# Sliding-window attention in a four-layer encoder: row sums of half the heads on VectorE instead of ScalarE's accumulator

## The reference, cut to what matters

```python
def swa_sink_mixer(h, w_in, sinks, w_out):
    ...
    s = jnp.einsum('bcqhgd,bckhd->bhgcqk', qc, kb) * (SW_HEAD ** -0.5)
    s = jnp.where(valid[:, None, :], s, -jnp.inf)
    sink = sinks.astype(F32).reshape(SW_KV_HEADS, SW_GROUP)[None, :, :, None, None, None]
    m = jnp.maximum(jnp.max(s, axis=-1, keepdims=True), sink)
    p = jnp.exp(s - m)
    p = p / (jnp.sum(p, axis=-1, keepdims=True) + jnp.exp(sink - m))
    o = jnp.einsum('bhgcqk,bckhd->bcqhgd', p, vb).reshape(B, T, SW_WIDTH)
    o = o * jax.nn.silu(g.astype(F32))
    return o.astype(h.dtype) @ w_out
```

## Time and profile before

| | |
|---|---|
| median of 3 runs | 1368.39 us |
| the profiled execution, its own time | 1368.35 us |
| its span, first to last instruction | 1366.5 us |
| TensorE busy | 1302.6 us, 95% |
| VectorE busy | 770.8 us, 56% |
| ScalarE busy | 429.2 us, 31% |
| GpSimd busy | 176.4 us, 13% |
| mean granted TensorE clock | 0.99 |

### The profile page before, as it was taken

How to read it: one execution, slowest core, us unless ns; L and a number is a source line. 1 busy time by engine, 2 the same in 40 slices (tenths; PEclk the granted TensorE clock), 3 DMA queues, 4 the chain that set the end, 5 groups by cost and what they waited for, 6 DMA issues and landing times. The chain is left out here.

```text
span 1366.5 us, 24895 instructions
## 1 busy us (share of the span) xinstructions
PE 1302.6 (95%) x10657; PEld 747.8 (55%) x10657; DVE 770.8 (56%) x1478; ACT 429.2 (31%) x1013; POOL 176.4 (13%) x168
## 2 busy tenths in 40 slices
PE   5999999999999999879999999899999999999998
PEld 3444444478746998754544446445444444468743
DVE  5676785966653333585444014424676785966653
ACT  3124166035302002561312062502123266035401
POOL 0000152010030243133000020000000153000000
PEclk9999999999999999989999999999999999999999
DMA  7222222100420223410222221113322222100221
GB/s 224 78 62 61 70 70 62 47 3 4 171 81 0 78 78 93 148 39 0 59 62 77 77 62 47 47 62 114 108 64 62 62 67 74 47 3 4 96 110 62
DMA packets 122270, 93.44 MB, mean 68 GB/s; under 512 B 5096, under 2 KB 112016, under 8 KB 121648
## 3 DMA queue, kind: packets, MB, share of 16 engines
q1 hardware_dynamic: 121456, 89.71, 21.9%
q10 hardware_dynamic: 704, 2.13, 0.4%
HBM read 85.54 MB, written 6.29 MB: 67 GB/s over the span
## 5 line engine op out<-in xcount | busy, mean ns | idle before, releaser
L1408 PE MATMUL bank<-arena 128*128 128x512 f32 x960 | 420.3, 595 | 1.5 <-ACT arena L995 1.5
L1356 PE MATMUL bank<-arena 64*64 64x64 f32 (+8 forms) x6848 | 316.0, 246 | 14.8 <-issue 5.4
L1408 PEld LDWEIGHTS bank<-arena 128*128 128x128 f32 x960 | 179.9, 190 | 227.8 <-issue 216.3
L1356 PEld LDWEIGHTS bank<-arena 64*64 64x64 f32 (+4 forms) x6848 | 200.5, 133 | 129.8 <-issue 112.2
L172 ACT ACTIVATE arena<-arena 128x512 f32<-128x512 f32 x40 | 25.1, 630 | 210.9 <-DVE arena L1339 116.6
L366 PE MATMUL bank<-arena 128*128 128x128 f32 x672 | 76.3, 275 | 2.4 <-DVE arena L434 1.4
L366 PEld LDWEIGHTS bank<-arena 128*128 128x128 f32 x672 | 75.5, 192 | 3.1 <-issue 3.1
L1118 DVE SCALAR_TENSOR_TENSOR arena<-arena 128x512 f32<-128x512 f32 x96 | 73.3, 810 | 0.0
L2165 PE MATMUL bank<-arena 128*128 128x512 f32 (+1 forms) x160 | 66.0, 571 | 0.3 <-PEq L730 0.3
L1021 ACT ACTIVATE arena<-arena 32x128 f32<-32x128 f32 x128 | 54.3, 424 | 36.8 <-DVE arena L1140 34.1
L2584 PE MATMUL bank<-arena 128*128 128x512 f32 x128 | 56.2, 593 | 0.9 <-DVE arena L2632 0.9
(11 more groups left out here) (255 smaller groups left out, 1594.8 us busy)
## 6 DMA issues: line engine op xcount, KB each, us to landing
arena<-in_rw_w_in SPq DMA_DIRECT2D x66, 512.0 KB, 4.1
arena<-in_ml_w_in SPq DMA_DIRECT2D x24, 512.0 KB, 3.9
arena<-in_sw_w_in SPq DMA_DIRECT2D x20, 512.0 KB, 4.7
arena<-in_rw_w_out SPq DMA_DIRECT2D x16, 512.0 KB, 7.0
spill<-arena SPq DMA_DIRECT2D x2, 2048.0 KB, 9.3
arena<-spill SPq DMA_DIRECT2D x2, 2048.0 KB, 14.0
arena<-in_sw_w_out SPq DMA_DIRECT2D x4, 1024.0 KB, 10.4
arena<-in_ml_w_out SPq DMA_DIRECT2D x8, 512.0 KB, 3.7
```

Of the source, the lines that this page charges most:

```text
L1356: mm = lambda out, a, b, start=True, stop=True: nc.tensor.matmul(out, a, b, start=start, stop=stop, skip_group_check=True)
L1408: last = nc.tensor.matmul(bank[:, :], slot[:, k, :], mix_at[what][:, k, :], start=k == 0, stop=k == KT - 1)
```

## The change

In `exps`, heads 0 to 3 are written without the accumulator output, and each counts a new semaphore, `half_exp`. In `normalise`, VectorE waits for the four, sums their probabilities over the keys in one instruction (128x4 numbers from 128x512; in chunk 0 from 128x256), and waits for its own result (`link`) before the addition. Heads 4 to 7 are as before. Below line 1739 every line number is higher afterwards: L1944 becomes L1952, L1946 becomes L1954, L1934 becomes L1940.

```diff
--- before.py
+++ after.py
@@ -1736,6 +1736,7 @@
     def block_of_g(j, below, right):
         return G[:, j + 4 * right, 256 * below:256 * below + 256]
 
+    s_early = m.sem("half_exp")
     keys = lambda c: C if c == 0 else P
     count = [0]
     with nc.Block() as block:
@@ -1871,8 +1872,13 @@
                 nc.scalar.activation(st[:, 2, :], st[:, 1, :], ACT.Exp)
                 for h in range(8):
                     bank = B[2 * (c % 2) + h % 2]
-                    last = nc.scalar.activation(p[:, h, 0:keys(c)], bank[:, P * (h // 2):P * (h // 2) + keys(c)], ACT.Exp,
-                                                bias=st[:, 0, h:h + 1], scale=C ** -0.5, accum_out=st[:, 3, h:h + 1])
+                    scores_of = bank[:, P * (h // 2):P * (h // 2) + keys(c)]
+                    if h < 4:
+                        last = nc.scalar.activation(p[:, h, 0:keys(c)], scores_of, ACT.Exp, bias=st[:, 0, h:h + 1],
+                                                    scale=C ** -0.5).then_inc(s_early.handle, 1)
+                    else:
+                        last = nc.scalar.activation(p[:, h, 0:keys(c)], scores_of, ACT.Exp, bias=st[:, 0, h:h + 1],
+                                                    scale=C ** -0.5, accum_out=st[:, 3, h:h + 1])
                 last.then_inc(s_exp.handle, 1)
 
             def evac(c):
@@ -1940,6 +1946,8 @@
 
             def normalise(c):
                 st, p = small[c % 2], prob[c % 2]
+                dve.wait_ge(s_early.handle, s_early.at(4 * c + 4))
+                link(nc.vector.tensor_reduce(st[:, 3, 0:4], p[:, 0:4, 0:keys(c)], AX.X, ALU.add))
                 dve.wait_ge(s_exp.handle, s_exp.at(c + 1))
                 link(nc.vector.tensor_tensor(st[:, 3, :], st[:, 3, :], st[:, 2, :], ALU.add))
                 link(nc.vector.reciprocal(st[:, 3, :], st[:, 3, :]))
@@ -2015,7 +2023,7 @@
             gate(NC - 1)
     seven.finish(SW_UNITS)
     for s, n in ((sig_done, 4), (g_used, 4), (turned, 10),
-                 (turn_evac, 10), (chain, count[0]), (sink, 64), (rotated, 6), (s_done, NC), (s_max, NC), (s_exp, NC),
+                 (turn_evac, 10), (chain, count[0]), (sink, 64), (rotated, 6), (s_done, NC), (s_max, NC), (s_exp, NC), (s_early, 4 * NC),
                  (normed, NC), (p_turned, 2 * NC), (p_evac, 2 * NC), (o_done, NC), (o_evac, NC)):
         s.base += n
```

## The result

| | kernel before | changed kernel |
|---|---|---|
| median | 1366.47 us (16 runs, 1364.74 to 1371.21) | 1372.17 us (16 runs, 1368.22 to 1376.27) |
| ratio to before | | 1.0032, 95% interval 1.002 to 1.0045 |
| the profiled execution | 1368.35 us | 1372.45 us |
| its span | 1366.5 us | 1370.6 us |

The change makes the kernel slower by 0.32%, 4.4 us (2.7 to 6.2) by the ratio; the two medians lie 5.7 us apart. The forecast was 1370.9 us, slower by 2.5 us over the 1368.39 known then, in a range of 1369.2 to 1374.0. The time lies in the range and the direction holds; but the profile shows rival 1, not the forecast, with rival 2 on top.

A forecast was written before the change was run, and what follows sets the result against it. TensorE bounds the kernel (busy 1302.6 of 1366.5 us), waiting on VectorE in the attention loop. Maxima(7) 1.7 us later plus sum(6) 0.72 delay the tail about 2.5: 1368.4 + 2.5 = 1370.9, range 1369.2 to 1374.0.

The forecast's parts named there:

- rival 1: Chunk 3: GpSimd starts first, holding VectorE's addition, then its multiply; +4.3 us at the end, 1372.7; chance 0.25.
- rival 2: Idle before the transposes of chunk 6: TensorE's granted clock falls, 2.0 us more, 1372.9; chance 0.13.
- That VectorE and not ScalarE sets the path of this loop: Attention loop over eight chunks: ScalarE waits for VectorE's maxima, 8.0 us; VectorE waits for exps only 2.0 us.
- The sum at 0.72 us with its link: VectorE, each chunk: the new sum of 512 elements to 4 plus one link costs 0.72 us, between 0.64 and 1.23.
- The accumulator's read at 0.09: ScalarE's exps: each dropped accumulator read saves 0.09 us, 0.37 a chunk, counting only in chunk 2.
- The sum of chunk 2 hidden: Chunk 2 on VectorE: its sum runs beside the last four exps; its addition moves from 580.45 to 580.80.
- Chunk 3's addition due at 585.71: VectorE in chunk 3: sum starts at 584.99, addition 0.72 later at 585.71, multiply would start at 586.14.
- GpSimd at 585.73: GpSimd's first subtraction starts at 585.73, when the last output weights have landed; the change does not move it.
- the 8-element addition (585.71) just passes first: Chunk 3: VectorE's addition precedes GpSimd by a margin of 0.02 us; only the multiply is held, ending at 591.46.
- The forecast's own case: Chunk 3: addition passes, multiply waits for GpSimd; transposes of chunk 6 2.4 to 2.5 us later, 1370.9; chance 0.42.
- Rivals 3 to 5: 3: GpSimd's end not moved, 1369.8, chance 0.12; 4: ScalarE sets pace, 1366.2, 0.06; 5: sums vanish, 1368.4, 0.02.

The follow-up runs named there:

- ScalarE's part alone: Changed kernel without VectorE's sums: accumulators of heads 0 to 3 left out, nothing in their place; ratio 0.9993 to the kernel before.
- VectorE's part alone: Changed kernel with its sums, while ScalarE keeps all eight accumulators; ratio 1.0034 to the kernel before.
- GpSimd behind chunk 3: Changed kernel with GpSimd's weight subtractions waiting until the multiply of chunk 3 is done; ratio 1.0023 to the kernel before.
- the idle transposes: Changed kernel with 16 idle transposes on TensorE in the gap before the transposes of chunk 6; ratio 1.0018 to the kernel before.
- one wait on GpSimd: Kernel before with GpSimd's two weight subtractions waiting until all eight chunks are normalised; ratio 0.9952 to the kernel before.
- GpSimd after all chunks: Changed kernel with GpSimd's two weight subtractions waiting until all eight chunks are normalised; ratio 0.9968 to the kernel before.

## Why the prediction was right or wrong, point by point

- That VectorE and not ScalarE sets the path of this loop: right. ScalarE's part alone gave 0.42 us at chunk 6, VectorE's part alone the time of the changed kernel.
- The sum at 0.72 us with its link: right, 0.68 out of SBUF and 0.03 behind it, the same as the maximum out of PSUM. The accumulator's read at 0.09: right, exps 0.25 us apart.
- The sum of chunk 2 hidden, its addition 0.35 late: right. It is 0.42 late in the loop (580.18 - 556.81 = 23.37 against 22.95).
- Chunk 3's addition due at 585.71, 28.21 in the loop: it came at 28.26. GpSimd at 585.73, 28.23: it came at 28.13.
- **The step that failed** is "the 8-element addition (585.71) just passes first". A margin of 0.02 us was no ground for calling it the likeliest, with a GpSimd start that scatters from 27.88 to 29.12, and lay between 27.88 and 28.28 in nine of eleven profiles. Four of the five profiles with that order of work show rival 1. It was priced at +4.3 us at the end of the chain; the transposes of chunk 6 came 4.35 late.
- The forecast's own case exists, and its working held where it occurred (transposes 2.14 late against 2.4).
- Rival 2, the clock: it fell in three profiles of the changed kernel, and cost 1.7 us where I had 2.0. It came together with rival 1, a sum that I had not given as a case of its own: 4.35 + 1.7 = 6.0 us in the profiles, against 4.4 (2.7 to 6.2) by the ratio of the timed runs and 5.7 between their medians.
- Rivals 3 to 5: GpSimd's end did move in the forecast's case; nothing became faster; nothing vanished.
- The level: the prediction stood on 1368.39 from three runs; over 16 runs it was 1366.47. In absolute time this hid part of the error: 1370.9 against 1372.17, but 2.5 against 4.4 (5.7 between the medians) as a difference.
- Luck: the time lies in the range because the range reached up to rivals 1 and 2, each taken alone, and because the level fell by 1.9 us. On 1368.39, the 5.7 us between the medians would have made 1374.1, just outside. The order of events that the forecast added up was not the one that the changed kernel's three profiles show.

On what the Trainium skill says (SBUF — State Buffer, Who interferes with whom): the trace agrees that the engine that issues first holds the other for a whole instruction, for inputs of 8 elements as for 1024 (4.40 and 5.36 us). But one input does not by itself free an instruction from the hold: the scaling has one and is held in the kernel before (2.47 us) and, with GpSimd behind chunk 3 and with the idle transposes, for 2.81 and 2.59 us, while the reciprocal with one is not (0.20 beside GpSimd's first, with the idle transposes). That a sum out of SBUF is not held no run here shows: none fell beside GpSimd.

## What to carry to other kernels

Before work is moved onto an engine, read from the waits whose instruction the others wait for in that loop, and not the shares of busy time. Where another engine's work holds yours for microseconds (4.5 us at a time here), ask which instruction will be next when that hold begins: a delay of 1.1 us (the addition of chunk 3 from 27.14 to 28.26 in the loop) decided here between holding the maxima of a later chunk and holding the probabilities that TensorE waits for. And if a long hold sits in such a loop at all, try moving it out before trimming the loop: one wait on GpSimd gave 6.6 us here by the ratio, while four accumulators fewer on ScalarE gave nothing that could be measured.

## What was not expected of the hardware

- A VectorE instruction that is held gets in between two back-to-back operations of GpSimd, though these are only 0.07 to 0.09 us apart: with the multiply queued, GpSimd's second took 5.40 us instead of 4.49.
- The same idle of 2.68 us in front of the same transposes was followed by a fall of TensorE's clock in three profiles of the changed kernel (2.67 and 2.68 us) but not in the one profile of the version that keeps the accumulators, nor in that of the changed kernel with GpSimd after all chunks (2.68 us in both). What decides between them no run here shows.
- The last of four DMAs of 1 MB, requested 14.8 to 15.6 us after the unit's start, landed at 27.7 to 28.1 us in nine profiles and at 28.8 and 29.0 in two. The three in front of it each landed within 0.4 us in all eleven.
